# Expert activations of a mixture of experts, transposed in 32 by 32 blocks on VectorE instead of on TensorE

## What is computed

```python
def moe_ffn(h, comb, wg, wu, wd):
    out = jnp.zeros_like(h)
    for e in range(N_EXPERTS):
        ye = (jax.nn.silu(h @ wg[e]) * (h @ wu[e])) @ wd[e]
        out = out + comb[:, e:e + 1].astype(h.dtype) * ye
    return out
```

## Time and profile before

| | |
|---|---|
| median of 3 runs | 1032.35 us (1032.21 to 1035.29) |
| the profiled execution | 1030.09 us |
| its span, first to last instruction | 1028.1 us |
| PE busy | 985.4 us, 96% of the span |
| DVE busy | 385.5 us, 37% |
| ACT busy | 235.2 us, 23% |
| GpSimd busy | 139.8 us, 14% |
| moved by DMA | 237.62 MB, 230.85 MB of it on SP's queue |

### The profile page before, as it was taken

One profiled execution on the slowest core, in us unless ns is written; L12 is line 12 of the kernel. 1 busy time (PEld: TensorE's weight loads), 2 busy tenths in 40 slices (PEclk: granted clock), 3 DMA queues, 4 the chain that ended last, 5 costly groups with the idle time before them and its releaser, 6 DMA issues.

```text
span 1028.1 us, 20300 instructions
## 1 busy us (share of the span) xinstructions
PE 985.4 (96%) x8539; PEld 745.2 (72%) x8539; DVE 385.5 (37%) x853; ACT 235.2 (23%) x467; POOL 139.8 (14%) x230
## 2 busy tenths in 40 slices
PE   5999999999999999999999999997899999999995
PEld 2667666666666666666666677665889999999981
DVE  3121234677257986656540611226110100101016
ACT  2240122233363322242251300002320111101013
POOL 0000132342020443224300000000100000000010
PEclk8999999999999999999999999998999999999998
DMA  9853344564355555646542633432839999999984
GB/s 378 318 213 121 125 164 144 193 231 174 136 201 202 217 208 198 234 156 227 185 143 85 255 123 123 164 117 77 313 140 385 398 410 400 416 386 420 395 335 131
DMA packets 47155, 237.62 MB, mean 231 GB/s; under 512 B 6800, under 2 KB 11248, under 8 KB 23792
## 3 DMA queue, kind: packets, MB, share of 16 engines
q1 hardware_dynamic: 45120, 230.85, 59.9%
q0 software_dynamic: 1520, 5.34, 1.5%
q10 hardware_dynamic: 448, 0.50, 0.2%
HBM read 212.31 MB, written 24.36 MB: 230 GB/s over the span
## 4 chain that ended last, share of the span: by engine, by line
PE 90%; DVE 4%; ACT 2%; DMA 1%; issue 1%; POOL 1%; DVEq 0%; SPq 0%; ACTq 0%; POOLq 0%
PE pjB L827 16%; PE pjA L827 15%; PE states L1364 11%; PE pjA L1212 7%; PE pjB L1212 7%; PE states L1367 5%; PE pjB L1364 3%; PE pjA L1364 3%; PE states L836 2%; PE pjA L1367 1%; PE pjB L1367 1%; PE bank L1176 1%; PE bank L951 1%; PE states L1191 1%; PE states L951 1%
## 5 line engine op out<-in xcount | busy, mean ns | idle before, releaser
L827 PE MATMUL pjB<-hF,ring 128*128 128x320 f32 x608 | 173.5, 439 | 0.0
L827 PE MATMUL pjA<-hF,ring 128*128 128x320 f32 x608 | 171.9, 436 | 0.5 <-ACT regA L1610 0.5
L1367 PE MATMUL states<-ring,oF 128*32 128x384 f32 x1392 | 154.6, 491 | 0.0
L1364 PE MATMUL states<-ring,oF 128*32 128x128 f32 x1392 | 154.4, 273 | 0.0
L1364 PEld LDWEIGHTS states<-ring,oF 128*32 128x32 f32 x1392 | 151.9, 110 | 0.2 <-issue 0.2
L827 PEld LDWEIGHTS pjB<-hF,ring 128*128 128x128 f32 x608 | 114.4, 192 | 49.2 <-issue 5.9
L827 PEld LDWEIGHTS pjA<-hF,ring 128*128 128x128 f32 x608 | 113.3, 190 | 50.5 <-issue 7.0
L2606 DVE TENSOR_TENSOR oF<-oF,states 128x384 f32<-128x384 f32 x15 | 8.3, 554 | 151.1 <-PE states L1367 151.1
L2336 DVE TENSOR_TENSOR G<-G 128x320 f32<-128x320 f32 x32 | 48.8, 1562 | 0.0
L1948 POOL TENSOR_TENSOR G<-regA,G 128x128 f32<-128x128 f32 (+1 forms) x32 | 19.0, 593 | 196.8 <-ACT G L1666 196.8
L1367 PE MATMUL pjB<-ring,hF 128*32 128x384 f32 x360 | 42.2, 493 | 0.0
(11 more groups left out here) (508 smaller groups left out, 1418.8 us busy)
## 6 DMA issues: line engine op xcount, KB each, us to landing
ring<-in_w SPq DMA_DIRECT2D x171, 1024.0 KB, 8.1
G<-in_ss SPq DMA_DIRECT2D x16, 512.0 KB, 4.0
out_ss_new<-G SPq DMA_DIRECT2D x16, 512.0 KB, 2.7
G<-csd SPq DMA_DIRECT2D x16, 320.0 KB, 3.4
G<-in_sg SPq DMA_DIRECT2D x4, 1024.0 KB, 6.3
out_sg_new<-G SPq DMA_DIRECT2D x16, 256.0 KB, 2.9
yd<-hF SPq DMA_DIRECT2D x14, 288.0 KB, 6.4
rF<-in_w SPq DMA_DIRECT2D x2, 1024.0 KB, 9.9
```

What stands on the lines that cost most here:

```text
L827: mm = pe.matmul(pj[g % 2][:, 0:T], w[:, k, half * P:half * P + P], hF[:, k, :], start=(k == 0), stop=(k == KT - 1))
L1364: pe.matmul(bank[CAP:P, c * P:(c + 1) * P], rows(c, True), w[:, WIDE:512], start=first and c == 0, stop=last, tile_position=(0, CAP), skip ...
L1367: mm = pe.matmul(bank[QUAD * c:QUAD * c + QUAD, 0:WIDE], rows(c, False), w[:, 0:WIDE], start=first, stop=last, tile_position=(0, QUAD * c) ...
```

## The change

PE no longer turns the activations of experts 0 to 14. DVE reads `actE` and writes `actT` in SBUF itself, with 16 `transpose` instructions an expert: for each destination group q of 32 partitions and each source group c of 32 partitions one instruction that turns three 32 by 32 blocks (one for each k). The product of expert e waits for DVE's own last turn (`s_hev`) where it waited for PE (`s_rd`). Expert 15, whose turn has `last_down()` right behind it, keeps the way over PE and PSUM (`turned_last`).

```diff
@@ PE, down(e, back, turn) @@
                     mm.then_inc(s_used, 1)
-                    if turn and h == 0:
-                        turn_act(turn[0])
...
@@ PE, one(e, v), e == 0 @@
                             turn_tokens(t)
-                        turn_act(0)
...
@@ DVE, one(e, v), and the same line in last(e, v) @@
-                        dve.wait_ge(s_rd, GH + PAIRS + e)
+                        dve.wait_ge(s_hev, XROWS // P + e)
                     dve.tensor_tensor(actE, sgE, b[3][:, 0:WIDE], ALU.mult).then_inc(s_eac, 1)
...
@@ DVE, last(e, v) @@
-                    turned(e, v)
+                    turned_last(v)
...
@@ DVE, turned(e, v) @@
-                    dve.wait_ge(s_rd, GH + PAIRS + 1 + e)
+                    dve.wait_ge(s_eac, e + 1)
                     if not (isinstance(e, int) and e < 2):
                         moe_used(dve, e, 5, 2)
+                    for q in range(4):
+                        to = slice(QUAD * q, QUAD * q + QUAD)
+                        for c in range(4):
+                            at = slice(QUAD * c, QUAD * c + QUAD)
+                            rows = slice(QUAD * c, QUAD * c + QUAD) if c < BLOCKS else slice(CAP, P)
+                            ins = dve.transpose(actT[to, v, :, rows],
+                                                actE[at, :].rearrange("p (k f) -> p k f", f=P)[:, :, QUAD * q:QUAD * q + QUAD])
+                    ins.then_inc(s_hev, 1)
+
+                def turned_last(v):
+
+                    dve.wait_ge(s_rd, GH + PAIRS + 1)
+                    moe_used(dve, E - 1, 5, 2)
                     dve.tensor_copy(actT[:, v], b[4][:, 0:WIDE].rearrange("p (k c) -> p k c", k=BLOCKS)).then_inc(s_hev, 1)
```

## The result

| | before | changed |
|---|---|---|
| median of 4 runs each, on one chip | 1032.28 us (1028.69 to 1035.29) | 1019.22 us (1017.86 to 1020.72) |
| ratio, with its 95% interval | | 0.9875 (0.984 to 0.9911) |
| the profiled execution | 1030.09 us | 1017.86 us |
| its span | 1028.1 us | 1015.9 us |
| PE busy | 985.4 us | 974.7 us |

What happened is, in the main, the rival *The loads keep up*. The times in this document are medians of executions at the usual clock; one of ten executions of the kernel with both turns took 1704.63 us, at a granted clock of 0.556, and is left out.

The account below looks back on a forecast made before the run. PE was taken to bound the kernel by a hair, 16.57 us an expert against DMA's 16.5. Of 12.3 us saved on PE, 4.95 - 1.4 = 3.6 us come through: 1032.35 - 3.6 = 1028.7 us, range 1023.5 to 1032.8.

Parts of the forecast that it names:

- The loads keep up: Rival, experts' loop: DMA follows PE, 15.7 us an expert by bytes, all 12.3 us come through, 1020.0 us; chance 0.13.
- six loads and two stores take DMA about 16.5 us: Experts' loop: DMA's own need per expert, almost exactly PE's 16.57 us, so PE is first by a hair.
- part 3: Weight loads in the loop: PE gains 0.85 us an expert for 7 experts, then waits for weights some 0.85 us each.
- Share 1.01: DMA's share from 860 to 880 us, in the experts' stage; said to be no proof of a full pipe.
- Landing of 8.9 us against 5.0: Loop loads against one issued on a short queue: about 3.9 us of other loads always ahead.
- An engine group that always has a queue delivers what it can.: Experts' loop: premise that always queued DMA runs at capacity, giving about 16.5 us an expert.
- Part 1: PE, experts' stage: loses 14 turns of 0.85 us and expert 0's 0.41 us, 12.3 us if nothing else becomes late.
- Part 2: DVE: loses 15 copies of 0.56 us, gets 240 turns of 0.26 us, 4.2 us an expert, hidden; cost 0.
- Part 4: End of the stage: PE can come 4.95 us earlier, gathers beside the last loads cost 1.4 us, leaving 3.6 us.
- The backlog reaches to the end: Rival, end of stage: expert 14's stores land behind SP's whole queue; 1 to 2.5 us gained, 1030.4 us; chance 0.23.
- The turns are dear: Rival, DVE: turns above 0.97 us each make DVE the bound, 1039 us at 1.0; chance 0.09 together with the clock.
- The clock: PE's clock falling in waits for weights; waits under a microsecond should not do it; chance 0.09 together with dear turns.

Follow-up runs that it names:

- the kernel with both turns: Changed kernel with PE's turns put back at their old places beside DVE's, PE's result unused for experts 0 to 14: 1032.96 us, ratio 1.0004 to the kernel before.

## Why the prediction was wrong

**The step that failed** is the sentence "six loads and two stores take DMA about 16.5 us", in the part on what bounds the kernel now, on which part 3 rests. The kernels with half of `down` left out show 15.82 us, and the last rounds with DVE's turns twice show it too. All else in part 3 follows from it: with 16.5 the spare lead of 6.3 us is used up after seven experts, with 15.82 it shrinks by 0.1 us an expert, some 1 us in the whole loop. Three readings led to the 16.5:

- *Share 1.01*. I noted that it is no proof of a full pipe, and gave that argument to the rival. It should have weighed more: 411 GB/s over 20 us against 426 in a clean stretch is 3.5%, 0.6 us of an expert's 16.57, and most of the 0.7 us in question. In these kernels the share does not fall when DMA has time left (1.00 at 394 GB/s over five experts with PE's turns twice), since some packets then take longer.
- *Landing of 8.9 us against 5.0*. I took the 3.9 us for other loads ahead. PE's turns twice shows that it does not drain with 1.1 us to spare in each expert.
- *"An engine group that always has a queue delivers what it can."* DMA's need was set equal to PE's period, 16.57, since neither fell behind the other. But equality is what any loop shows in which DMA follows PE, whatever DMA's need. The trace of before bounds it from above only. By the rows at hand the lower bound was 15.7, which the rival had, and the measured value lies close to that end. For an unknown between such bounds I took the upper one without a row that spoke for it. The rival had nearly the right number but not the right reason: no deeper queue closes the holes; they are the spare time itself, and go with it.

**Part 1** was right. PE gave 0.85 us an expert, 16.57 to 15.72, and PE's turns put back brought back all of the time. 12.3 us less the 0.7 us below make 11.6, and the profiled execution shows 11.5 (13.05 less the 1.5 us from ahead of the stage); the two timed comparisons gave 13.1 and 10.9 us, and their intervals hold it (0.9891 +- 0.0025 is 8.7 to 13.7 us).

**Part 2** was right in the price (0.27 us against 0.26) and for experts 0 to 13. It missed one place: I let `down(e)` always follow `gate_up(e + 1)`, though the order of the last experts, as I had described it myself, puts `down(14)` ahead of `gate_up(15)`. There the cover is two halves of `down(13)`, 5.24 us, against 0.55 + 4.51 us and what lies between them. Its chunk is 3.27 us behind the last one in place of 2.62 (966.50 to 969.77): 0.7 us. The kernel with DVE's turns twice makes a wait of 4.77 us of it.

**Part 4** did not come into play as written, since PE never used its lead up. Of its pieces, gathers do run beside the last load, from 984.03 us, and the last two loads land after 10.5 and 11.6 us in place of 9.6; they were issued so early that 4 us were left. Expert 14's store on ACT's queue, issued at 976.16, had landed at 983.8, ahead of the load that SP had issued at 975.50 (987.1). So these stores did not wait behind SP's whole queue, against the rival *The backlog reaches to the end*; the trace before has the same order, with the store of 989.21 landing at 998.0 and the load of 988.55 at 999.6.

**The turns are dear**: no. **The clock**: the waits under a microsecond in the experts' loop left it at 1.00, as said there, and so did those of up to 1.4 us in each expert with half of `down` left out (1.00 from 900 to 940 us). In the waits of 4.8 and 5.2 us of the experiments it fell.

The Trainium skill, "DMA: Bandwidth & Descriptors", section "Where 436 GB/s comes from", gives 435 GB/s for the fabric and about 358 GB/s as binding for loads from DRAM. The measured ceiling of this loop, 423 GB/s with its stores and 426 without, is 2 to 3% under the one and 18 to 19% over the other; 15.82 us an expert stands against the 15.4 that I had estimated from the first.

## What to carry to other kernels

As this loop shows, a busy share of 1.0 and a constant time to landing need not mean that DMA is full: divide the bytes of one round of the loop by the rate of a clean stretch, and where that is less than the round takes, the difference is spare. Where a forecast hangs on it, press the other engine, by leaving out some of its work, and read the new period. Before work is moved to an idle engine, look for the round in which its cover is thinner (the last ones, out of step with the loop), and price a PE wait of 5 us there with the slow matmuls behind it (2.2 to 2.5 us here).

## What the runs showed of the hardware

- **Stretched packets.** With 0.75 to 1.1 us an expert to spare, DMA does not go idle; it moves 282 to 340 GB/s for some 4 us at a share of 0.92 to 1.02. Why that comes just ahead of and behind the stores stays open. From my own reckoning of the 16 updates that a load makes of its semaphore: the first comes some 5.2 us after the issue of the load ahead of the stores in the kernel before, 6.2 to 6.7 in three executions of the changed one, and 10.3 to 11.5 with `down` halved; for a lone load it is 4.3. So the first of the 16 have next to nothing ahead of them in the kernel before. The spread from the first update to the last does not sort the kernels: it is 2.3 to 3.7 us from load to load in the kernel before, but 2.5, 2.1 and 2.3 in three executions of the changed one, and 2.1 and 3.5 in the two kernels with `down` halved. A kernel without stores would have told more; it wasn't tried.
- **Turns across partition groups.** DVE's transposes of 32 partitions by 96 elements took 266 to 275 ns each, whatever the groups of source and destination.
- **PE's clock.** In and behind waits of PE of 4.77 and 5.22 us the granted clock was half for some 6.8 us. In the changed kernel run again it was at half for 6.8 us from 732.9 us on, at the start of the experts' stage, and executions of one kernel differ by where and how often that happens: the kernel before had executions of 1028.6 to 1035.7 us. Differences of 3 us between two single executions say nothing here.
